# The scans of the even layer: denominators in groups of four, inter-tile scaling on ScalarE, decay rows by DMA

## What is computed

```
mLSTM      s   = (q k^T) * exp(dlog - m_t)          num = s v + w_int * (q C)
           den = sum(s) + w_int * (q n)             h   = num / max(|den|, exp(-m_t))
           C, n <- dec * (C, n) + (wg * k)^T (v, 1)
retention  s   = (q k^T) * decay                    o   = s v + xi * (q S)
           S   <- g_end * S + (zeta * k)^T v
both       the forward and the backward direction are summed
```

## Time and profile before

| | |
|---|---|
| median of 3 runs | 5341.34 us (5338.39 to 5348.19) |
| profiled execution | 5341.9 us, span 5340.2 us |
| mean granted TensorE clock | 0.959 of full speed |
| PE, DVE, ACT, POOL busy | 5007.7 (94%), 3170.6 (59%), 1436.8 (27%), 1499.5 us (28%) |
| the chain that ended last | PE 88%, DVE 6%, POOL 2% |

### The profile page before, as it was taken

The page is one execution under the profiler, slowest core; times in us unless marked ns, Lnnn a source line. Parts: engine busy times, 40 slices in busy tenths (PEclk is TensorE's granted clock), DMA queues, the critical chain, the costliest instruction groups (busy, mean ns, idle before and its releaser), DMA issues.

```text
span 5340.2 us, 62753 instructions
## 1 busy us (share of the span) xinstructions
PE 5007.7 (94%) x26071; PEld 4171.0 (78%) x26071; DVE 3170.6 (59%) x5163; ACT 1436.8 (27%) x1788; POOL 1499.5 (28%) x839
## 2 busy tenths in 40 slices
PE   5999779999999989999899999989999999899997
PEld 3767678888888878888666678988888888788886
DVE  2162568927888156666455541379828884366666
ACT  0110022224444222222222222022224443222222
POOL 0020222332232274542011110023332223555531
PEclk8979889999999999999799999999999999999999
DMA  7141012334555578886210011012335554588873
GB/s 300 64 167 63 20 72 76 126 119 146 182 166 177 208 258 299 296 300 242 87 38 33 32 44 48 32 66 101 130 119 169 173 178 162 217 315 296 298 299 139
DMA packets 275268, 835.37 MB, mean 156 GB/s; under 512 B 24434, under 2 KB 157810, under 8 KB 214566
## 3 DMA queue, kind: packets, MB, share of 16 engines
q1 hardware_dynamic: 67104, 520.91, 25.8%
q10 hardware_dynamic: 162824, 176.07, 10.0%
q0 software_dynamic: 45056, 134.38, 7.4%
HBM read 674.40 MB, written 156.80 MB: 156 GB/s over the span
## 4 chain that ended last, share of the span: by engine, by line
PE 88%; DVE 6%; POOL 2%; DMA 1%; ACT 1%; issue 1%; SPq 0%; ACTq 0%; DVEq 0%; POOLq 0%
PE PS L593 20%; PE PS L594 20%; PE PS L595 20%; PE PS L742 3%; PE PS L438 3%; PE PS L855 3%; PE PS L833 3%; PE PS L498 3%; PE PS L662 2%; PE PS L817 2%; POOL A L1901 1%; PE PS L585 1%; DVE EP L1388 1%; DMA ring<-in_w_mod 1%; PE PS L739 1%
## 5 line engine op out<-in xcount | busy, mean ns | idle before, releaser
L1889 POOL TENSOR_TENSOR wL<-raw,wH 128x2048 fp32r<-128x2048 f32 x144 | 668.2, 4641 | 1541.1 <-ACT wH L1610 1541.1
L593 PE MATMUL PS<-hH,wH 128*128 128x512 f32 (+1 forms) x2560 | 964.6, 377 | 29.5 <-DVE hL L1142 28.5
L594 PE MATMUL PS<-hL,wH 128*128 128x512 f32 (+1 forms) x2560 | 960.9, 375 | 0.0
L595 PE MATMUL PS<-hH,wL 128*128 128x512 f32 (+1 forms) x2560 | 959.7, 375 | 0.0
L1610 ACT ACTIVATE wH<-raw 128x2048 fp32r<-128x2048 f32 x272 | 520.6, 1915 | 1055.5 <-PE PS L595 1047.2
L595 PE MATMUL PS<-wH,WL 128*128 128x512 f32 x2048 | 802.1, 392 | 0.0
L593 PEld LDWEIGHTS PS<-hH,wH 128*128 128x128 f32 x2560 | 484.0, 189 | 101.2 <-issue 29.2
L1263 DVE TENSOR_TENSOR wL<-raw,wH 128x2048 fp32r<-128x2048 f32 x128 | 293.3, 2291 | 449.6 <-ACT wH L1610 449.6
L595 PEld LDWEIGHTS PS<-hH,wL 128*128 128x128 f32 x2560 | 483.1, 189 | 82.7
L594 PEld LDWEIGHTS PS<-hL,wH 128*128 128x128 f32 x2560 | 483.9, 189 | 69.6
L1909 POOL DMA_INDIRECT ubuf<-in_v,idxV x256 | 361.6, 1412 | 574.0 <-DVE acc L1275 529.8
(11 more groups left out here) (349 smaller groups left out, 8107.8 us busy)
## 6 DMA issues: line engine op xcount, KB each, us to landing
raw<-in_u SPq DMA_DIRECT2D x128, 1024.0 KB, 6.5
raw<-in_v SPq DMA_DIRECT2D x128, 1024.0 KB, 4.9
expert_acts<-abuf ACTq DMA_DIRECT2D x128, 512.0 KB, 3.2
expert_gates<-wide ACTq DMA_DIRECT2D x64, 1024.0 KB, 6.5
wide<-expert_acts SPq DMA_DIRECT2D x64, 1024.0 KB, 5.7
ring<-in_w_mod SPq DMA_DIRECT2D x48, 1024.0 KB, 9.0
wide<-expert_gates SPq DMA_DIRECT2D x16, 2048.0 KB, 11.7
gb<-expert_gates SPq DMA_DIRECT2D x16, 2048.0 KB, 11.8
```

The costliest lines, as they stand in the source:

```text
L593: nc.tensor.matmul(out, lhsH, rhsH, start=start, stop=False)
L594: nc.tensor.matmul(out, lhsH, rhsL, start=False, stop=False)
L595: return nc.tensor.matmul(out, lhsL, rhsH, start=False, stop=stop)
L1889: G.tensor_tensor(wL[:, n % NSPLIT, :], raw[:, n % NRAW, :], wH[:, n % NSPLIT, :].bitcast(f32), ALU.subtract).then_inc(lo_u, 1)
```

## The change

The decay rows are stored to DRAM once and loaded per unit, broadcast over the partitions, into one of four buffers `eb`, by ScalarE's queue three units ahead; the `sel4` products of the scan go. ScalarE scales the inter-tile part: for the mLSTM into `nd`, now with eight buffers (in the memory of the rows), for the retention units that write first directly into `f`. VectorE adds the intra-tile part in place; the second writers of the retention scan add both parts straight into `f`. The mLSTM denominators are formed for four units in one set of four instructions, and the quotient of a unit is taken four units later; TensorE's H waits for the sum (`num_done`), no more for the quotient. The last four quotients follow the loop. Semaphores, their declarations and the unchanged lines are left out of the diff.

```diff
+NEB = 4
+    rowd = nc.dram_tensor("decay_rows", [NH, 2, T], f32, kind="Internal").ap()
-    row = sb("row", [NH, 2, T], scope=ev)
+    rown = sb("rown", [P, 2 * T], scope=ev)
+    row = rown[0:NH, :].rearrange("p (d t) -> p d t", d=2)
+    nd = rown[:, 0:4 * NH // 2 * (DH + 2)].rearrange("p (u w) -> p u w", w=DH + 2)
-    eb = sb("eb", [P, 2, P], scope=ev)
+    eb = sb("eb", [P, NEB, P], scope=ev)
-    nd = sb("nd", [P, 2, DH + 2], scope=ev)
+    GROUP = NH
+    BY_ACT = [u for u, (s, h, d) in enumerate(UNITS) if s > 0 and first_on(s, d)]
...
@@ TensorE, scan loop
-                            if fam == 0:
-                                last = nc.tensor.matmul(PS[:, i % 2, P:2 * P], sel4[:, h, :], row[:, d, t * P:(t + 1) * P],
-                                                        start=True, stop=True)
...
-                                pe.wait_ge(h_done, fam * NU + u - 1)
+                                pe.wait_ge(num_done if fam == 0 else h_done, fam * NU + u - 1)
...
@@ VectorE
+                    def denominators(n):
+                        s, h0 = n // 2, 2 * (n % 2)
+                        g = n % 2 * GROUP
+                        group = nd[:, g:g + GROUP, :].rearrange("p (h d) w -> p h d w", d=2)
+                        ve.wait_ge(num_done, (n + 1) * GROUP)
+                        link(V.scalar_tensor_tensor(nd[:, g:g + GROUP, DH + 1], nd[:, g:g + GROUP, DH], -1.0, nd[:, g:g + GROUP, DH], ALU.mult, ALU.max))
+                        for d in range(2):
+                            do(V.tensor_tensor(group[:, :, d, DH + 1], group[:, :, d, DH + 1], cols[:, tile_of(s, d), 3, d, h0:h0 + 2], ALU.max))
+                        settle()
+                        link(V.reciprocal(nd[:, g:g + GROUP, DH + 1], nd[:, g:g + GROUP, DH + 1]))
+                    def quotient(u):
+                        s, h, d = UNITS[u]
+                        out = f[:, tile_of(s, d), h * DH:(h + 1) * DH]
+                        ndu = nd[:, u % (2 * GROUP), :]
+                        if first_on(s, d):
+                            V.tensor_scalar(out, ndu[:, 0:DH], ndu[:, DH + 1:DH + 2], None, ALU.mult).then_inc(h_done, 1)
+                        else:
+                            ve.wait_ge(h_done, earlier(u) + 1)
+                            V.scalar_tensor_tensor(out, ndu[:, 0:DH], ndu[:, DH + 1:DH + 2], out, ALU.mult, ALU.add).then_inc(h_done, 1)
...
-                                if i >= 2:
-                                    ve.wait_ge(p_ready, i - 1)
-                                V.scalar_tensor_tensor(eb[:, i % 2, :], PS[:, i % 2, P:2 * P], cols[:, t, 2, d, h:h + 1], mask[:, d, :],
+                                ve.wait_ge(row_full[i % NEB], 16 * (i // NEB + 1))
+                                V.scalar_tensor_tensor(eb[:, i % NEB, :], eb[:, i % NEB, :], cols[:, t, 2, d, h:h + 1], mask[:, d, :],
...
-                        if s > 0:
-                            w = cols[:, t, 1, d, h:h + 1] if fam == 0 else xz[:, 0, d, h:h + 1]
-                            do(V.tensor_scalar(ndu[:, 0:width], inter, w, None, ALU.mult))
+                        if fam == 1 and not first_on(s, d):
+                            ve.wait_ge(h_done, NU + earlier(u) + 1)
+                            if s > 0:
+                                do(V.scalar_tensor_tensor(out, inter, xz[:, 0, d, h:h + 1], out, ALU.mult, ALU.add))
...
+                        if fam == 0:
+                            ndu = nd[:, u % (2 * GROUP), 0:width]
...
+                            if s == 0:
+                                V.tensor_copy(ndu, num).then_inc(num_done, 1)
+                            else:
+                                ve.wait_ge(inter_ready, u - 2 * NH + 1)
+                                V.tensor_tensor(ndu, ndu, num, ALU.add).then_inc(num_done, 1)
+                            if u >= GROUP:
+                                quotient(u - GROUP)
+                            if u % GROUP == GROUP - 1:
+                                denominators(u // GROUP)
+                        elif first_on(s, d):
+                            if s == 0:
+                                V.tensor_copy(out, num).then_inc(h_done, 1)
+                            else:
+                                ve.wait_ge(inter_ready, NU - 2 * NH + BY_ACT.index(u) + 1)
+                                V.tensor_tensor(out, out, num, ALU.add).then_inc(h_done, 1)
                         else:
...
+                            settle()
+                            V.tensor_tensor(out, out, num, ALU.add).then_inc(h_done, 1)
+                    if fam == 0:
+                        for u in range(NU - GROUP, NU):
+                            quotient(u)
+                    ve.wait_ge(h_done, (fam + 1) * NU)
...
@@ ScalarE
+                        act.dma_start(rowd, row[:]).then_inc(row_stored, 16)
...
+                        def inter_rows(u):
+                            s, h, d = UNITS[u]
+                            act.wait_ge(products, at["H", 0, u])
+                            act.wait_ge(h_done, u - 2 * GROUP + 1)
+                            S.activation(nd[:, u % (2 * GROUP), 0:DH + 1], PS[:, 2 + u % 2, 256:256 + DH + 1], ACT.Copy,
+                                         scale=cols[:, tile_of(s, d), 1, d, h:h + 1]).then_inc(inter_ready, 1)
+                        act.wait_ge(cols_ready, 1)
+                        def row_load(u):
+                            s, h, d = UNITS[u]
+                            t = tile_of(s, d)
+                            if u >= NEB:
+                                act.wait_ge(p_ready, u - NEB + 1)
+                            act.dma_start(eb[:, u % NEB, :], rowd[h, d, t * P:(t + 1) * P].partition_broadcast(P)).then_inc(row_full[u % NEB], 16)
+                        act.wait_ge(row_stored, 16)
+                        for u in range(NEB - 1):
+                            row_load(u)
                         for u in range(NU):
                             act.wait_ge(e_ready, u + 1)
-                            S.activation(eb[:, u % 2, :], eb[:, u % 2, :], ACT.Exp).then_inc(exp_ready, 1)
+                            S.activation(eb[:, u % NEB, :], eb[:, u % NEB, :], ACT.Exp).then_inc(exp_ready, 1)
+                            if u + NEB - 1 < NU:
+                                row_load(u + NEB - 1)
+                            if u - 2 >= 2 * NH:
+                                inter_rows(u - 2)
...
+                        for u in range(NU - 2, NU):
+                            inter_rows(u)
                         mod_copy(5)
...
+                        for u in BY_ACT:
+                            s, h, d = UNITS[u]
+                            act.wait_ge(products, at["H", 1, u])
+                            S.activation(f[:, tile_of(s, d), W_A + h * DH:W_A + (h + 1) * DH], PS[:, 2 + u % 2, 256:256 + DH], ACT.Copy,
+                                         scale=xz[:, 0, d, h:h + 1]).then_inc(inter_ready, 1)
```

More of the change, by code:

```diff
@@ L276, in trunk @@
     mod1_copied, mod1_rows, bias_full = sem("mod1_copied"), sem("mod1_rows"), sem("bias_full")
+    row_stored = sem("row_stored")
+    row_full = [sem(f"row_full{i}") for i in range(NEB)]
     c_ready, mod_evac, mod_rows, mod_cols = sem("c_ready"), sem("mod_evac"), sem("mod_rows"), sem("mod_cols")
@@ L284, in trunk @@
     e_ready, exp_ready, p_ready, kw_ready = sem("e_ready"), sem("exp_ready"), sem("p_ready"), sem("kw_ready")
+    inter_ready, num_done = sem("inter_ready"), sem("num_done")
     h_done, state_ready, ret_ready = sem("h_done"), sem("state_ready"), sem("ret_ready")
@@ L331, in first_on, with earlier @@
         return step < other or (step == other and d == 0)
+    BY_ACT = [u for u, (s, h, d) in enumerate(UNITS) if s > 0 and first_on(s, d)]
+    def earlier(u):
+        s, h, d = UNITS[u]
+        return [j for j in range(u) if UNITS[j][1] == h and tile_of(UNITS[j][0], UNITS[j][2]) == tile_of(s, d)][-1]
     def bc(v, n):
@@ L1047, in even @@
                                 ve.wait_ge(exp_ready, u + 1)
-                                w = eb[:, u % 2, :]
+                                w = eb[:, u % NEB, :]
                             else:
@@ L1071, in even @@
                             V.scalar_tensor_tensor(Cst[:, d, h, 0:width], Cst[:, d, h, 0:width], w, U, ALU.mult, ALU.add).then_inc(state_ready, 1)
-                        settle()
-                        if s > 0:
-                            link(V.tensor_tensor(ndu[:, 0:width], ndu[:, 0:width], num, ALU.add))
-                        else:
[L1076 to L1082, removed]
-                                V.tensor_scalar(out, ndu[:, 0:DH], ndu[:, DH + 1:DH + 2], None, ALU.mult).then_inc(h_done, 1)
-                            else:
-                                V.scalar_tensor_tensor(out, ndu[:, 0:DH], ndu[:, DH + 1:DH + 2], out, ALU.mult, ALU.add).then_inc(h_done, 1)
-                        elif first_on(s, d):
-                            V.tensor_copy(out, ndu[:, 0:DH]).then_inc(h_done, 1)
```

(11 more changed lines are left out.)

3 lines of the change are left out of this document (1 added, 2 removed).

## The result

The changed kernel takes 5293.65 us (median of 4 runs, 5291.39 to 5294.58), the kernel before, run on the same chip, 5339.86 us (5337.68 to 5348.19). The ratio is 0.9909, with a 95% interval of 0.9894 to 0.9923.

A forecast was written before the change was run, and what follows sets the result against it. The prediction took PE to bound the mLSTM scan and VectorE the retention scan. Savings of 5.8 + 8 + 9 + 0 + 0.7 + 3.5 + 8 = 35 us took 5341.9 to 5306.9, 5306 against the median; range 5292 to 5322.

The forecast's parts named there:

- Units 0 to 15: First part of the mLSTM scan: 5.8 us saved in units 0 to 7 and 8 us in units 8 to 15.
- VectorE's unit 1.55: mLSTM units 0 to 15: VectorE needs 1.25 us per unit plus 0.3 for grouped denominators, 1.55 us together.
- if the clock stays: mLSTM units 8 to 15: PE's clock stays at 0.50, saving 5.8 us; if it rises, 9.5; 8 taken.
- Units 16 to 39: mLSTM scan among the modulation pieces: 22 decay-row products at 0.41 us go; 9 us saved, from 4 to 13.
- Rows by DMA: Forty 64 KB row loads, three units ahead: landing in 2.5 us, 1.1 us per unit, so hidden.
- The prediction's own sign against this step: mLSTM exponent: a wait on `decay_rows` there, with landings over 4 us, would refute the row step.
- The loop (x + 0.8)/3: mLSTM time per unit if a row lands in x us: 2.7 us at 7.4, slower from about x = 9.
- The rival of late rows: mLSTM row loads land late and the change is slower: 5346 us at a landing of 10 us; chance 0.05.
- End of the mLSTM scan: Last quotients, held again beside GpSimd: 0 us, at worst 2 lost, at best 7.6 won.
- the rival that freed them: End of the mLSTM scan: VectorE finishes four quotients before GpSimd starts, 7.6 us more, 5298; chance 0.09.
- The rule that spoke against the change: mLSTM exponent, now reading SBUF alone, contends with GpSimd's `kw` in 32 units: 4 us lost at most.
- Retention scan: Copies and additions go: 0.7 us in units 0 to 7, 3.5 in the middle 22, 8 in the last stretch.

The follow-up runs named there:

- the run with two 128-row pairs: Changed kernel with two 128-row products per mLSTM unit (S twice more, read by nobody) put behind S: 5303.1 us, ratio 0.9909–0.9942.
- the rows alone: Kernel before with only the decay rows by DMA into four buffers and the 4-row product gone, VectorE's work as before: 5323.6 us.
- the vector part alone: Changed kernel with decay rows back on PE (4-row product, no row loads), grouped denominators, late quotients, ScalarE's scaling and new retention scan kept: 5319.6 us.
- the run with the late `og` product: Changed kernel with GpSimd's last modulation addition and its mLSTM `og` product put behind the scan: 5284.1 us, ratio 0.9875–0.9905.

## Why the prediction fell 12 us short

*Units 0 to 15 (13.8 predicted, 19.7 measured): the step that failed, in two terms.* The mechanism was right (4-row pair off PE, VectorE next). First, "VectorE's unit 1.55" was too long. Its terms were 1.25 for the ordinary part and 1.2 per group of denominators; they measure 1.13 and 0.77, so 1.32 to 1.35. The 1.2 held the way to the first step (0.28) beside the ordinary unit's own link to the next exponent (0.27), and only one of the two is there; the rest of it, 0.94, was taken from the links of the 128x1 steps, and is the 0.77. Second, "if the clock stays" got nearly half the weight, so that 8 stood between 5.8 and 9.5. The clock was 1.00 from about 272 on, and the run with two 128-row pairs shows that it stays there under more PE work than the change left. With both terms right the sum is 8 x (2.31 - 1.35) + 8 x (2.74 - 1.35) = 18.8. That the low clock belonged to the pair that went could be asked of the rows (the retention scan at 1.00 has the same products without it), and the prediction named that row but gave it only half the weight.

*Units 16 to 39 (9 predicted; 9.6 to the end of the last modulation piece, 11.1 to the last P).* Right in size, and the quotient wait was replaced by the wait for ScalarE's copies, as the working had it. But two misses cancel in it, which is luck: PE's busy time fell by 15.2 us (78.37 to 63.14) and not by 9.0, and its idle time, put at no change, grew by 5.6 (11.3 to 17.0). A group of denominators was held by an addition three times, for 2.3 us each, and not once for 0.9. The share was less clean too: the rows alone bring 9.5 of the 11.1 and the vector part alone 6.5, while waits for the weights and for GpSimd's additions stay in this stretch.

*Rows by DMA: hidden (2.5 us taken; 3.2 median).* Nearly right, with less margin than thought. The prediction's own sign against this step did come: VectorE waited for `decay_rows` four times, 3.4 us in all, and 13 of the 40 loads took over 4 us to land, up to 11.1, all of them beside the weights. What the waits cost is small, since six buffers take them all away for 1.8 us. The loop (x + 0.8)/3 gives 1.33 us at 3.2, no less than VectorE's unit, and three buffers show the step beyond. The rival of late rows didn't come.

*End of the mLSTM scan: 0 (0.9 from the end of the last modulation piece).* Right, a quotient was held again, for 8.03 us, the second of the last four and not the first; the rival that freed them didn't come, and the run with the late `og` product shows the 7.6 us that it priced (7.8).

*The rule that spoke against the change.* The exponent L1072 now has its operands in SBUF alone, and its forty instances took 352 ns at the median, as the 0.35 us of the earlier trace rows. Fifteen of them ran beside a `kw`: thirteen took 0.35 us and two 0.44 and 0.46, so the 4 us at most shrank to 0.2, though a `kw` beside them took up to 0.94 us where 0.62 is the median. The Trainium skill's rule ("SBUF — State Buffer", section "Who interferes with whom") is borne out by the quotients and by the sums of the retention scan. The section limits its second half, on instructions with at most one SBUF input, to those outside the 2-port modes, which the prediction left out. It matters here: one-operand TENSOR_SCALARs were held, L1149 above for 2.01 us, and in the kernel before two quotients L1083 for 1.93 beside an addition of 2.33. Whether they ran in such a mode, no row shows.

*Retention scan (12.2 predicted, 17.0 measured): the other step that failed.* The hold vanished as argued: the sums have one operand in PSUM. The unit was taken as 1.15 from "eight matmuls of 24.69/176 = 0.14 us", but this mean came from a stretch in which PE waited for VectorE; unhindered the pairs take 0.22 (the state update's 0.45 in every other unit), and the unit is 21.53/21 = 1.03. Units up to the tenth saved 1.4 (0.7 predicted for eight), the middle 6.3 (3.5 predicted), the end 9.3 (8 predicted).

5.9 and 4.8 us account for 10.7 of the 12. The two scans together shrank by 47.3 us, inside the 20 to 49 that the prediction allowed itself, and by the medians (46.2) no gain came from outside them.

## What to carry to other kernels

Price the next engine from the distance between starts of its instructions, count each link between two of them once, and take an engine's floor from a stretch in which it never waits: the mean taken here where it waits was too long (0.14 us a matmul against 21.02/168 = 0.125). When a removed instruction and a low granted clock stand in the same stretch, make the clock a term of its own with both levels, and test it with a dummy that nobody reads. After each bound that falls, ask which instructions of VectorE and GpSimd now meet: here moving GpSimd's `og` product behind a scan (in one kernel with the addition ahead of it) gave 8 to 11 us for one wait.

## What was not expected of the hardware

- With a single 4-row product per unit, beside three or four of 128 rows, the granted clock stayed at 0.50 for 36 us with PE busy throughout; one or two 128-row products in its place ran at 1.00, also where PE was busy for 3.00 of 3.00 us. Among the modulation pieces the same 4-row product went with 0.78 to 0.84.
- A hold by GpSimd spanned two instructions that follow each other: one 128x128 quotient took 8.03 us beside an addition of 2.33 and a product of 5.56. BN_STATS with one operand ran at 0.2 us each beside the same two, and sums with one operand in PSUM were not held at all, but a TENSOR_SCALAR with one operand in SBUF was held up to the product's end (2.01 us instead of 0.34).
- A 64 KB broadcast from DRAM to 128 partitions landed in 2.8 us at best and 3.2 at the median, but in up to 11.1 where the modulation weights were loading, at 280 GB/s in all.
